# Softmax denominators of windowed attention: one 128x8 transpose and eight row DMAs in place of a spread copy and four transposes

## The reference

```python
s = jnp.einsum('bqhgd,bkhd->bhgqk', qb, kk).astype(jnp.float32) * scale      # masked by the window
p = jax.nn.softmax(jnp.concatenate(parts + [sink], axis=-1), axis=-1)        # sink: one logit per head
o = jnp.einsum('bhgqk,bkhd->bqhgd', p[..., start:start + n], vv)             # summed over window and context
```

## Time and profile before

| | us |
|---|---|
| median of 3 runs | 2724.66 (2721.68 to 2724.75) |
| the profiled execution | 2726.17 |
| its span, first to last instruction | 2723.6 |
| TensorE busy | 2614.6 (96%) |
| VectorE busy | 2012.8 (74%) |
| ScalarE busy | 1359.3 (50%) |
| GpSimd busy | 613.1 (23%) |
| attention stage | about 253 to 520 of the span |
| mean granted TensorE clock | 0.985 |

### The profile page before, as it was taken

How to read it: one execution, slowest core, us unless ns; L and a number is a source line. 1 busy time by engine, 2 the same in 40 slices (tenths; PEclk the granted TensorE clock), 3 DMA queues, 4 the chain that set the end, 5 groups by cost and what they waited for, 6 DMA issues and landing times. The chain is left out here.

```text
span 2723.6 us, 44405 instructions
## 1 busy us (share of the span) xinstructions
PE 2614.6 (96%) x14920; PEld 1176.8 (43%) x14923; DVE 2012.8 (74%) x5303; ACT 1359.3 (50%) x3150; POOL 613.1 (23%) x467
## 2 busy tenths in 40 slices
PE   7999999999899999999999889998999999999996
PEld 2444666544433333333444365444333343333342
DVE  4996666585588887788888465855898888888875
ACT  1112666343256666666666251431666666666651
POOL 0000000111023233233322221100233323233322
PEclk9999999999999999999999999999999999999998
DMA  9776500200399999999999732016999999999996
GB/s 366 266 266 200 187 17 17 76 39 39 146 371 368 332 337 353 327 337 377 352 334 339 248 146 84 39 47 241 362 366 340 343 318 341 335 372 332 338 345 205
DMA packets 151614, 697.65 MB, mean 256 GB/s; under 512 B 25505, under 2 KB 30881, under 8 KB 99162
## 3 DMA queue, kind: packets, MB, share of 16 engines
q1 hardware_dynamic: 103964, 555.09, 52.3%
q0 software_dynamic: 46832, 136.58, 20.3%
q10 hardware_dynamic: 592, 3.16, 0.3%
HBM read 597.50 MB, written 129.13 MB: 267 GB/s over the span
## 5 line engine op out<-in xcount | busy, mean ns | idle before, releaser
L1842 ACT ACTIVATE xT<-xt_blocks 32x256 f32<-32x256 f32 x2176 | 900.4, 414 | 39.0 <-DVE xt_blocks L1663 11.6
L1920 PE MATMUL exG<-ring,xT 128*32 128x512 f32 (+2 forms) x2608 | 572.1, 593 | 1.3 <-DMA ring<-in_exp_w_up_dram 0.7
L1678 DVE STREAM_TRANSPOSE ex_hT<-ex_h 32x64 f32<-32x64 f32 x2240 | 528.7, 236 | 33.6
L1920 PE MATMUL exG<-wide_w,xT 128*32 128x512 f32 (+2 forms) x1472 | 385.2, 600 | 0.7 <-DVE xT L1657 0.7
L1589 POOL DMA_INDIRECT y_scratch<-wide_w,idx_out x203 | 335.8, 1654 | 149.0 <-issue 66.6
L1920 PE MATMUL exG<-wide_t,xT 128*32 128x512 f32 (+2 forms) x960 | 361.5, 603 | 7.8 <-issue 4.4
L1576 POOL DMA_INDIRECT wide_t<-u_scratch,idx x144 | 152.6, 1060 | 937.8 <-DVE idx_out L1714 742.5
L1920 PEld LDWEIGHTS exG<-ring,xT 128*32 128x32 f32 (+2 forms) x2608 | 199.5, 129 | 314.7 <-issue 312.2
L1854 ACT ACTIVATE ex_e<-exG 128x256 f32<-128x256 f32 x142 | 54.4, 383 | 503.7 <-PE exG L1920 500.2
L1955 PE MATMUL exD<-ring,ex_hT 128*32 128x512 f32 (+2 forms) x1304 | 296.2, 597 | 2.5 <-DVE wide_w L1706 2.5
L1668 DVE TENSOR_TENSOR ex_h<-ex_e,exG 128x256 f32<-128x256 f32 x142 | 86.7, 611 | 190.9 <-ACT ex_e L1854 162.3
(11 more groups left out here) (369 smaller groups left out, 3275.8 us busy)
## 6 DMA issues: line engine op xcount, KB each, us to landing
ring<-in_exp_w_gate_dram SPq DMA_DIRECT2D x64, 1024.0 KB
ring<-in_exp_w_up_dram SPq DMA_DIRECT2D x64, 1024.0 KB
ring<-in_exp_w_down_dram SPq DMA_DIRECT2D x64, 1024.0 KB
wide_t<-in_exp_w_gate_dram SPq DMA_DIRECT2D x34, 1024.0 KB
wide_t<-in_exp_w_up_dram SPq DMA_DIRECT2D x34, 1024.0 KB
wide_t<-in_exp_w_down_dram SPq DMA_DIRECT2D x34, 1024.0 KB
wide_w<-in_exp_w_gate_dram SPq DMA_DIRECT2D x32, 1024.0 KB
wide_w<-in_exp_w_up_dram SPq DMA_DIRECT2D x32, 1024.0 KB
```

The lines of the kernel that those rows point to most:

```text
L1678: last = dve.transpose(hT[m * UNIT:(m + 1) * UNIT, par].rearrange("p (k t) -> p k t", k=FK)[:, :, a * UNIT:(a + 1) * UNIT], hid[a * UNIT:( ...
L1842: last = act.activation(xT[m * UNIT:(m + 1) * UNIT, par, :, a * UNIT:(a + 1) * UNIT], parts[a * UNIT:(a + 1) * UNIT, m], ACT.Copy)
L1920: last = pe.matmul(psG[par][p:p + m], xT[:, par, k, p:p + m], ring[s % RING][:, 0:2, k * FF:(k + 1) * FF], start=k == 0, stop=k == KT - 1)
```

## The change

The reciprocals `den` (128 x 8) are turned in one transpose into 8 rows of `psR`; ScalarE copies these to `den_rows` (8 x 128, `lift`); and SyncE issues eight DMAs, one for each head, each of which reads one partition of `den_rows` 64 times and writes 64 partitions of `share`, 512 bytes each. `divide` waits for all eight (`share_in`, 16 a DMA). GpSimd's copy is gone. The zero rows are no longer issued in one go: `clear(n)` issues one of the nine behind the eight DMAs of round n, for n = 0 to 8; the loads of q tiles stand ahead of the odd rounds' `share_of`.

```diff
@@ -708,7 +708,7 @@
                 mx, nm = sb("mx", [P, 2, 2]), sb("nm", [P, H])
                 rs, es, den = sb("row_sum", [P, H]), sb("sink_exp", [P, H // 2]), sb("den", [P, H // 2])
                 share = sb("share", [P, 4, P])
-                spread = sb("den_spread", [P, 4, 2, HD])
+                den_rows = sb("den_rows", [8, P])
                 prob = sb("prob", [P, 2, 2, S])
                 pT = sb("pT", [P, 2, 4, S])
                 zero = logits[:].rearrange("p t e -> p (t e)")
@@ -720,8 +720,8 @@
                 far_mm, score_mm, max_done, exp_done = sem("far_mm"), sem("score_mm"), sem("max_done"), sem("exp_done")
                 T_first, T_rest, copied_a, copied_d, pv_mm, o_done = (sem(n) for n in (
                     "probT_first", "probT_rest", "probT_a", "probT_d", "pv_mm", "o_done"))
-                sink_in, sink_done, den_own, den_done, spread_done, den_mm, share_done = (sem(n) for n in (
-                    "sink_in", "sink_done", "den_own", "den_done", "den_spread_done", "den_mm", "share_done"))
+                sink_in, sink_done, den_own, den_done, den_mm, den_lifted, share_in = (sem(n) for n in (
+                    "sink_in", "sink_done", "den_own", "den_done", "den_mm", "den_lifted", "share_in"))
 
                 def heads(p):
 
@@ -758,29 +758,40 @@
                                 first = (2 * c + a) * 4 * HD
                                 sp.dma_start(w_o[a * HD:(a + 1) * HD, 4 * c:4 * c + 4],
                                              A["attn_w_o"][0, first:first + 4 * HD].rearrange("(i p) n -> p i n", p=HD)).then_inc(w_in, 16)
+                        def clear(n):
+                            if n == 0:
+                                sp.dma_start(u_dram[DUMMY:, :].rearrange("p (h c) -> p h c", h=2),
+                                             zero.unsqueeze(1).to_broadcast([P, 2, D // 2])).then_inc(zero_out, 16)
+                                return
+                            l, j, h = (n - 1) // 4, (n - 1) // 2 % 2, (n - 1) % 2
+                            half = y_dram[l].rearrange("(n p j) (h c) -> j h p n c", p=P, j=2, h=2)
+                            if j == 1:
+                                sp.dma_start(half[1, h], zero.unsqueeze(1).to_broadcast([P, YROWS // P, D // 2])).then_inc(zero_out, 16)
+                            else:
+                                sp.dma_start(half[0, h, :, NT], zero).then_inc(zero_out, 16)
+
+                        def share_of(n):
+                            sp.wait_ge(den_lifted, n + 1)
+                            at_least(sp, o_done, n)
+                            for h in range(8):
+                                a, i = divmod(h, 4)
+                                sp.dma_start(share[a * HD:(a + 1) * HD, i],
+                                             den_rows[h:h + 1].unsqueeze(1).to_broadcast([1, HD, P])).then_inc(share_in, 16)
                         sp.wait_ge(zeroed, 1)
-                        sp.dma_start(u_dram[DUMMY:, :].rearrange("p (h c) -> p h c", h=2),
-                                     zero.unsqueeze(1).to_broadcast([P, 2, D // 2])).then_inc(zero_out, 16)
-                        for l in range(DEPTH):
-                            half = y_dram[l].rearrange("(n p j) (h c) -> j h p n c", p=P, j=2, h=2)
-                            for h in range(2):
-                                sp.dma_start(half[1, h], zero.unsqueeze(1).to_broadcast([P, YROWS // P, D // 2])).then_inc(zero_out, 16)
-                                sp.dma_start(half[0, h, :, NT], zero).then_inc(zero_out, 16)
-                        for t in range(2, NT):
-                            sp.wait_ge(score_mm, PAIRS * (t - 1))
-                            load(t)
+                        for n in range(2 * NT):
+                            if n % 2 == 1 and n + 3 < 2 * NT:
+                                t = (n + 3) // 2
+                                sp.wait_ge(score_mm, PAIRS * (t - 1))
+                                load(t)
+                            share_of(n)
+                            if n < 1 + 4 * DEPTH:
+                                clear(n)
                         sp.wait_ge(w_in, 64)
                         sp.wait_ge(zero_out, 16 + 64 * DEPTH)
 
                     @block.gpsimd
                     def _(pool):
                         pool.memset(zero, 0.0).then_inc(zeroed, 1)
-                        pool.wait_ge(zeroed, 1)
-                        for n in range(2 * NT):
-                            pool.wait_ge(den_done, n + 1)
-                            at_least(pool, den_mm, n)
-                            pool.tensor_copy(spread[:], den[:].rearrange("p (a i) -> p i a", a=2).unsqueeze(3).to_broadcast([P, 4, 2, HD])
-                                             ).then_inc(spread_done, 1)
 
                     @block.vector
                     def _(dve):
@@ -821,14 +832,14 @@
                             c = n % 2
                             dve.wait_ge(sink_done, n + 1)
                             dve.wait_ge(exp_done, 8 * n + 8)
-                            at_least(dve, spread_done, n)
+                            at_least(dve, den_mm, n)
                             dve.tensor_tensor(es[:], rs[:, 8 * c:8 * c + 8], es[:], ALU.add).then_inc(den_own, 1)
                             dve.wait_ge(den_own, n + 1)
                             dve.reciprocal(den[:], es[:]).then_inc(den_done, 1)
 
                         def divide(n):
                             t, c = n // 2, n % 2
-                            dve.wait_ge(share_done, n + 1)
+                            dve.wait_ge(share_in, 128 * n + 128)
                             dve.wait_ge(pv_mm, 4 * n + 4)
                             dve.tensor_tensor(oT[:, 4 * c:4 * c + 4, t * P:(t + 1) * P], psO[:], share[:], ALU.mult).then_inc(o_done, 1)
 
@@ -873,10 +884,10 @@
                             act.wait_ge(sink_in, n + 1)
                             act.activation(es[:], es[:], ACT.Exp).then_inc(sink_done, 1)
 
-                        def shares(n):
+                        def lift(n):
                             act.wait_ge(den_mm, n + 1)
-                            at_least(act, o_done, n)
-                            act.activation(share[:], psR[:], ACT.Copy).then_inc(share_done, 1)
+                            at_least(act, share_in, 128 * n)
+                            act.activation(den_rows[:], psR[0:8, 0], ACT.Copy).then_inc(den_lifted, 1)
 
                         exps(0)
                         for p in range(N):
@@ -884,10 +895,10 @@
                             if p % 4 == 2:
                                 sinks(p // 4)
                             if p >= 4 and p % 4 == 0:
-                                shares(p // 4 - 1)
+                                lift(p // 4 - 1)
                             if p + 1 < N:
                                 exps(p + 1)
-                        shares(N // 4 - 1)
+                        lift(N // 4 - 1)
 
                     @block.tensor
                     def _(pe):
@@ -956,11 +967,9 @@
                             last.then_inc(pv_mm, 1)
 
                         def denominators(n):
-                            pe.wait_ge(spread_done, n + 1)
-                            at_least(pe, share_done, n)
-                            for i in range(4):
-                                last = pe.transpose(psR[:, i], spread[:, i].rearrange("p a d -> p (a d)"), ident[:])
-                            last.then_inc(den_mm, 1)
+                            pe.wait_ge(den_done, n + 1)
+                            at_least(pe, den_lifted, n)
+                            pe.transpose(psR[0:8, 0], den[:], ident[:]).then_inc(den_mm, 1)
 
                         scores(0)
                         scores(1)
```

## The result

The changed kernel takes 2836.95 us (median of 6 runs, 2833.23 to 2840.99), the kernel before 2724.7 beside it. The ratio is 1.041, with a 95% interval of 1.0396 to 1.0423. The forecast was 2855 with a range of 2725 to 2880. The profiled execution took 2835.69 us, its span is 2833.9, 110.3 more than before.

What follows compares the result with a forecast made beforehand. TensorE was taken to bound the attention stage. Gain -5.0, twelve inner rounds +96.0, three edge rounds +27.3 and the end +12.4 make +130.7 us: 2855 us on the median, range 2725 to 2880.

Steps and rivals of the forecast that it cites:

- The bound, and the gain: Attention stage: TensorE bounds it; one transpose for four saves 0.33 us a round in rounds 0 to 14, 5.0 us.
- (a) Issue: SyncE issuing the eight share DMAs: 0.55 us each (0.36 to 0.67), the eighth starting 3.85 us after the first.
- (b) Latency: Share DMAs: 1.6 us from issue to landing, read from the last f_ny copy of 4 KB.
- (c) The bytes: Share DMAs: 32.8 KB out of one partition at 25.4 GB/s take 1.29 us, eight take 10.3 us.
- in order: DMA queue: transfers run one after another without overlap, as read from w_o's two halves; eight in order take 10.3 us.
- Where it meets the loop: Landing 11.9 us after the first issue, 6.3 us late in inner rounds and 7.4 in edge rounds; TensorE waits.
- The clock: TensorE idles 5.4 us in a late round, so its granted clock falls, costing 1.7 us (0 to 3.7).
- The end: Last round: divide starts 9.4 us later, and the fallen clock costs the next stage 3.0 us more.
- Zero rows and loads: SyncE's queue: zero rows behind the share DMAs and the moved q loads cost nothing, hidden by 10 us of slack.
- The sum: Whole kernel: gain, inner rounds, edge rounds and end together add 130.7 us, giving 2855 us on the median.
- B (latency only): Rival: one partition feeds all engines, 0.16 us a transfer; +0.8 us, 2725.5 us, holding up to 5.6 us landing; chance 0.33.
- C (two groups at once): Rival: rows 0 to 3 and 4 to 7 are served at once, landing in 9.0 us; 2780 us, chance 0.17.

Runs made afterwards that it cites:

- e1: Changed kernel without its eight DMAs, share set to 1 once, division by the denominators left out; attention stage 260.4 us, against 266.8 in the kernel before.
- e2: Changed kernel with each of the eight DMAs reading 64 partitions of the identity, denominators left out; attention stage 280.0 us, against 376.8 in the changed kernel.
- e3: Changed kernel with the eight rows on partitions 0, 4, 8 to 28 instead of 0 to 7; 2759.7 us, ratio 1.0125 to the kernel before.
- e11: Changed kernel with its eight DMAs issued in head order 0, 4, 1, 5, 2, 6, 3, 7; 2759.5 us, ratio 1.0121 to the kernel before.
- e12: Changed kernel with each zero-row DMA issued only once the divide of its round is done; 2827.0 us, ratio 1.0367 to the kernel before.
- e5: Changed kernel with 36 spare transposes on TensorE in each of its 15 waits for divide; 2815.3 us, ratio 1.0321 to the kernel before.

## Why the prediction was right, point by point

- **The bound, and the gain** held: 0.32 us a round (e1), 6.4 in the stage in place of 5.9.
- **(a) Issue** was sized at 0.55 us. It is 0.62 in e2 and e3, where nothing holds the queue, 0.76 in the changed kernel (6.06 for eight), hidden under the bytes as forecast. In e2, e3 and e11 it is no longer hidden.
- **(b) Latency** of 1.6 us: e2 has 1.9 at the median, in which 32.8 KB are moved (0.16 us by the forecast's own lower bound). That leaves 1.74: right within 0.15. The 2.0 us that the prediction quotes from the Trainium skill stand there in the section on DMAs that GpSimd issues; SyncE issues these.
- **(c) The bytes**: 1.29 us a transfer, 10.3 for eight. Measured are 11.58 us in all with zero rows behind and 10.56 without; less 1.6 of latency that is 1.25 and 1.12 a transfer. The rate for one place is right (25 GB/s), and e2 shows that it is the source. The reason "in order" was too wide: what I read out of `w_o`'s two halves in the earlier trace rows, that transfers to different places don't overlap when they are queued together, is refuted by e3 and e11. It came out nearly right here only because the kernel issues its rows 0 to 3, which share one limit, one behind the other, and that was luck. The row shows less than I took from it: the loop over the halves is the outer one, so `w_o`'s four DMAs stand in the queue as two for the one half and then two for the other, like rows 0 to 3 and rows 4 to 7. Different halves are neighbours once only, and the rate rises there as it does in e12, for about 1 us. In the kernel before:

```profile
264.00:265.00 1.00, 0.84 (x8) 0.69 (x8) 0.60 (x2) 0.44 (x2) 0.00 (x0) 1.00 1.03 197
...
265.00:266.00 1.00, 1.00 (x10) 0.53 (x6) 0.45 (x1) 1.00 (x4) 0.00 (x0) 1.00 1.05 229
...
266.00:267.00 1.00, 0.99 (x8) 0.62 (x8) 1.00 (x3) 0.25 (x3) 0.00 (x0) 1.00 1.05 209
```

Some 20 to 30 KB more than before and after it are moved in that us, against some 40 in e12's. For a transfer of 32.8 KB that is about all of it, for one of 1 MB nothing. That both are the same effect is a reading of these windows; no run varies the size.
- **Where it meets the loop**: forecast 6.3 late in an inner round; the landing came 0.3 sooner (11.58 for 11.9), and `divide` waited for what the order of the queues said, values and turn behind it. A round grew by 7.24 us; forecast 8.0 - 0.33 = 7.67. In e5, whose clock holds, inner rounds with zero rows behind take 22.3 us (rounds 2 to 4), against e1's 16.45 without DMAs: 5.8 late, where 6.3 was forecast.
- **The clock**: it fell in each of the 15 rounds, for 6.8 us in thirteen and for 3.4 in rounds 11 and 14. 1.7 us a round was forecast; e5 gives back 1.95 in rounds 1 to 10 and 1.5 over all; 3.0 was forecast for the next stage, 2.92 measured.
- **The end**: forecast `divide` 9.4 later, measured from the start of the last reciprocal 7.9 (618.34 to 629.85, 11.5 us, against 3.6 in the earlier trace rows). The last round has no zero rows behind it, so its landing took 10.56 and not 11.9. (Of the forecast's own figures, 528.3 - 518.97 is 9.3.)
- **Zero rows and loads**: costed at nothing, worth 10 us (e12). This is the one term that was missed altogether. It hid behind the bytes, which were 1.3 us a round too high (11.9 for the 10.56 of a round with nothing behind) for want of the overlap at row 4: in nine rounds the two errors cancel to 0.3 us. That the forecast of the landing was so close is in part luck.
- **The sum**: +130.7 forecast, +112.9 measured (110.0 in the stage, 2.9 behind it). Most of the difference is in the rounds. From the first lift (274.38) to the last (618.99) it is 344.6 us, from GpSimd's first copy before (272.14) to its last (515.65) 243.5: +101.1 for fifteen rounds, where 12 x 7.67 + 3 x 8.77 = 118.4 was forecast. The nine rounds with zero rows behind grew by 6.9 to 7.3 (the first one by 8.9), and so did round 10, which has a q load behind; rounds 9 and 11 to 14 have nothing behind and grew by 3.8 to 6.6. (With 0 for the clock the forecast's low end is 2855 - 15 x 1.7 = 2829.5 and not 2833; the measured 2837 lies above both.)
- **The rivals**: B (latency only) is what e2 does, and there it costs 13 us in the stage, not 1, since 0.62 of issue in place of 0.55 and 1.9 in place of 1.6 pass the limit of 5.6 us. C (two groups at once) happened in the changed kernel only where the queue passes from row 3 to row 4, but it is e11: 7.7 us, where C said 9.0, and a run of 2759.5, where C said 2780. Against C the prediction had only `w_o`'s halves, whose order in the queue it overlooked.

## What to carry to other kernels

A DMA that copies one partition of SBUF to many is bound by the place that it reads, at some 25 GB/s here; if it must be, take neighbours in the queue from partitions four apart, or read the row from DRAM. Before moving a step of 0.6 us onto DMAs, compare the time from the first issue to the last landing (here 7 x 0.62 + 1.9 = 6.2 us even with 64 source partitions) with the slack of the wait at its end; the gain (0.32 us a round) was real, and it only showed in the run once the wait was put three pairs later with a second buffer and the last round was left as it had been. And waits of TensorE as long as these (4.2 to 5.9 us) are paid twice, the second time through the clock; in e3, where 14 waits come to 21.5 us, the clock stayed up in most rounds.

## What the runs showed of the hardware that I had not expected

Small DMAs in one queue do overlap, if neighbours in it read different groups of four partitions: 51 GB/s in alternating order against 25 in plain order, where the two groups meet for about 1 us only. A DMA queued behind a batch delays its landing, with 2304 KB by 1.0 us of 11.6. Spare transposes in TensorE's waits made the kernel 22 us faster by keeping the clock. And two loads that read 4 KB of DRAM 64 times over land 2.9 us after their issue at the median, 262 KB in all, where the eight DMAs out of SBUF need 10.6 to 11.6 us from the first issue.
